# The dilated mixer worked through by head pairs, with its attention two rounds behind its projections

## The reference, cut to what matters

```python
proj = (h @ w_in).reshape(B, S, 3, 3, 16, 64)           # 3 groups; q, k, v; 16 heads of 64
for gi, (window, dilation) in enumerate(((128, 1), (512, 4), (2048, 16))):
    q = rms_norm(proj[:, :, gi, 0], g_q[gi]); k = rms_norm(proj[:, :, gi, 1], g_k[gi])
    v = proj[:, :, gi, 2]
    o, lse = dilated_group(q, k, v, pos, rel_bias[:, gi*16:gi*16+16], window, dilation)
# the three groups are merged by a softmax over their lse: one softmax over all their keys
o = einsum('gbsh,gbshd->bshd', softmax(stack(lses)), stack(outs))
x = x + gate1 * (o.reshape(B, S, 1024) @ w_o)
```

## Time and profile before

| | us |
|---|---|
| median of 3 runs | 2176.52 |
| lowest, highest | 2175.99, 2177.66 |
| the profiled execution, its own time | 2172.89 |
| its span, first to last instruction | 2170.0 |
| busy: PE, PE weight loads, DVE, ACT | 2015.7, 1865.3, 1442.6, 1103.1 |

### The profile page before, as it was taken

One profiled execution on the slowest core, in us unless ns is written; L12 is line 12 of the kernel. 1 busy time (PEld: TensorE's weight loads), 2 busy tenths in 40 slices (PEclk: granted clock), 3 DMA queues, 4 the chain that ended last, 5 costly groups with the idle time before them and its releaser, 6 DMA issues.

```text
span 2170.0 us, 34519 instructions
## 1 busy us (share of the span) xinstructions
PE 2015.7 (93%) x14140; PEld 1865.3 (86%) x14140; DVE 1442.6 (66%) x2525; ACT 1103.1 (51%) x1815; POOL 324.3 (15%) x339
## 2 busy tenths in 40 slices
PE   2758999889999998999889998999999999999998
PEld 1747999889998888999778898999999998888886
DVE  6696785656656655754764545899998775555554
ACT  3544553325655234543555444446777774444444
POOL 3020000000000000000000000004885980000000
PEclk7879999889999789999999999999999999999999
DMA  7534587525545103665432434454444445555553
GB/s 268 190 120 162 196 269 258 193 78 192 195 168 194 35 20 111 203 192 185 176 130 102 146 128 146 174 184 167 154 149 159 144 138 181 186 186 191 186 187 124
DMA packets 97086, 356.22 MB, mean 164 GB/s; under 512 B 10705, under 2 KB 10833, under 8 KB 96545
## 3 DMA queue, kind: packets, MB, share of 16 engines
q1 hardware_dynamic: 83824, 305.04, 40.9%
q0 software_dynamic: 12672, 48.08, 6.9%
q10 hardware_dynamic: 432, 0.90, 0.1%
HBM read 352.93 MB, written 1.05 MB: 163 GB/s over the span
## 4 chain that ended last, share of the span: by engine, by line
PE 83%; DVE 11%; ACT 4%; DMA 1%; issue 1%; SPq 0%; DVEq 0%; POOL 0%; ACTq 0%
PE psum L460 23%; PE psum L461 22%; PE psum L462 22%; PE psum L453 14%; DVE wl L1548 2%; PE psum L467 1%; DVE araw L1531 1%; ACT work L1028 1%; DMA first<-in_ada_w 1%; DVE work L1528 1%; ACT sqh L1028 1%; ACT wh L1040 0%; DVE first L1531 0%; DVE st L1538 0%; DMA araw<-in_ada_w 0%
## 5 line engine op out<-in xcount | busy, mean ns | idle before, releaser
L1548 DVE TENSOR_TENSOR wl<-raw,wh 128x1024 fp32r<-128x1024 f32 (+1 forms) x564 | 688.1, 1226 | 429.9 <-ACT wh L1040 429.3
L1040 ACT ACTIVATE wh<-raw 128x1024 fp32r<-128x1024 f32 (+1 forms) x564 | 592.9, 1053 | 437.0 <-PE psum L462 421.0
L460 PE MATMUL psum<-peer_hh,wh 128*128 128x256 f32 x1152 | 331.0, 287 | 4.2 <-DVE peer_hl L1520 4.0
L461 PE MATMUL psum<-peer_hl,wh 128*128 128x256 f32 x1152 | 326.1, 283 | 0.0
L462 PE MATMUL psum<-peer_hh,wl 128*128 128x256 f32 x1152 | 326.0, 283 | 0.0
L460 PEld LDWEIGHTS psum<-peer_hh,wh 128*128 128x128 f32 x1152 | 219.3, 190 | 5.4 <-issue 4.4
L462 PEld LDWEIGHTS psum<-peer_hh,wl 128*128 128x128 f32 x1152 | 217.2, 189 | 0.0
L461 PEld LDWEIGHTS psum<-peer_hl,wh 128*128 128x128 f32 x1152 | 217.2, 189 | 0.0
L460 PE MATMUL psum<-wh,csh 128*128 128x512 f32 x512 | 202.9, 396 | 0.0
L462 PE MATMUL psum<-wh,csl 128*128 128x512 f32 x512 | 202.7, 396 | 0.0
L461 PE MATMUL psum<-wl,csh 128*128 128x512 f32 x512 | 202.7, 396 | 0.0
(11 more groups left out here) (423 smaller groups left out, 4747.2 us busy)
## 6 DMA issues: line engine op xcount, KB each, us to landing
raw<-in_mlp_w SPq DMA_DIRECT2D x128, 512.0 KB, 4.2
raw<-in_eu SPq DMA_DIRECT2D x128, 512.0 KB, 3.2
raw<-in_ev SPq DMA_DIRECT2D x128, 512.0 KB, 3.2
araw<-in_ada_w POOLq DMA_DIRECT2D x80, 512.0 KB, 4.1
raw<-in_dil_qk SPq DMA_DIRECT2D x48, 512.0 KB, 4.1
raw<-in_dil_v SPq DMA_DIRECT2D x24, 512.0 KB, 4.4
first<-in_ada_w SPq DMA_DIRECT2D x8, 1024.0 KB, 18.1
raw<-in_w_in SPq DMA_DIRECT2D x16, 512.0 KB, 3.3
```

The source lines that it names most:

```text
L460: e.matmul(o, l[0], r[0], start=start, stop=False, skip_group_check=loose)
L461: e.matmul(o, l[0], r[1], start=False, stop=False, skip_group_check=loose)
L1040: e.activation(b.wh[v % NSPLIT][:, 0:cols], b.raw[v % NRAW][:, 0:cols], ACT.Copy).then_inc(S.hi, 1)
L1548: e.tensor_tensor(b.wl[v % NSPLIT][:, 0:cols], b.raw[v % NRAW][:, 0:cols], b.wh[v % NSPLIT][:, 0:cols].bitcast(F32), ALU.subtract).then_in ...
```

## The change

Work is ordered by the eight pairs of heads instead of by groups, by one list (`DIL_ORDER`) that PE, ACT and DVE all follow.
- First come 18 of the 24 value units, with both `bias(0)` and `bias(1)` beside them; `B` holds both query tiles. The other 6 value units come after the last q and k.
- Round c (0 to 7) has the six q and k units of pair c. In rounds 2 to 7 the four attention steps of pair c-2 stand behind its first two units, two behind each. The norm of pair c-1's heads is finished in round c: the three roots are taken in one go, and each of the three q/k banks is scaled by two instructions of 256 columns instead of one of 512.
- Round 8 has the 6 late value units and the norm of pair 7. Then come steps 24 to 34, with units of `dil_w_o` between them. Such a unit now takes the rows of `w_o` that belong to one pair, and adds to all eight output blocks, which keep four PSUM banks; the residual and the squares for the next norm come after the last unit.
- In a step, ACT copies the transposed probabilities first (one buffer, where there were three) and exponentiates second; PE takes `s3` ahead of `s2`.
- The mask is fetched whole by one transfer; ticks have places of their own in the list (31 of them).

```diff
 
 
+def dil_order():
+
+
+    values = [("dil_v", 8 * g + x, x // 2) for g in range(3) for x in range(8)]
+    out = []
+    for i, e in enumerate([e for e in values if e[2] < 3]):
+        out.append(e)
+        if i % 4 == 3:
+            out.append(("tick", 0, 0))
+    out.append(("biased", 0, 0))
+    late = [e for e in values if e[2] == 3]
+
+    def beside(c, z):
+
+        if z % 2 == 0:
+            s, g = (c, z // 2 - 1) if z else (c - 1, 2)
+            if 0 <= s < 8:
+                out.append(("sum", s, g))
+        s, g = {3: (c, 0), 5: (c, 1), 0: (c - 1, 2)}.get(z, (-1, 0))
+        if c and z == 3:
+            out.append(("root", c - 1, 0))
+        if c and z in (3, 4):
+            out.append(("root square", c - 1, z - 3))
+        if c and z == 4:
+            out.append(("root square", c - 1, 2))
+        if 0 <= s < 8:
+            out.append(("mean", s, g))
+        if z % 2 and c < 8:
+            out.append(("square", c, z // 2))
+        if z in (0, 2, 3):
+            out.append(("tick", c, z))
+        if c and z in (3, 4):
+            out.append(("scale", c - 1, z - 3))
+        if c and z == 4:
+            out.append(("scale", c - 1, 2))
+        for u in {0: (4 * c - 8, 4 * c - 7), 1: (4 * c - 6, 4 * c - 5)}.get(z, ()):
+            if 0 <= u < 24:
+                out.append(("step", u, 0))
+
+    for c in range(8):
+        for z in range(6):
+            out.append(("dil_qk", 8 * z + c, z))
+            beside(c, z)
+    for z in range(6):
+        out.append(late[z])
+        beside(8, z)
+    out += [("step", 24, 0), ("step", 25, 0)]
+    tail = [(26,), (27,), (28, 29), (30, 31), (32, 33), (34,), (), ()]
+    for i, steps in enumerate(tail):
+        out += [("step", u, 0) for u in steps] + [("dil_w_o", i, 0)]
+    return out
+
+
+DIL_ORDER = dil_order()
 PLAN = []
...
+    m.qk = sb("qk", 2 * 6 * 256, where=s).rearrange("p (b z t) -> p b z t", b=2, z=6)
+    with ExitStack() as values:
+        m.vtf = sb("vt", 8 * 768, where=values)
+        m.vt = m.vtf.rearrange("p (c g t n) -> p c g t n", c=8, g=3, t=2)
+    m.o = sb("dil_o", 8 * 768, F32R, s).rearrange("p (c x t) -> p c x t", c=8, x=3)
+    m.B = sb("B", 2 * 16 * 512, where=s).rearrange("p (t h n) -> p t h n", t=2, h=16)
+    m.work = sb("work", 2048, where=s)
+    with ExitStack() as early:
+        m.step = sb("step", 1024, F32R, early).rearrange("p (g q) -> p g q", g=8)
+        m.ot = sb("ot", 768, where=early)
+        m.maskc = sb("maskc", 1024, where=early)
+        m.tabs = pair("tabs", 192, early)
+        m.pF = sb("pF", 320, where=early)
+    m.hms = sb("head_means", 4 * 512, where=s).rearrange("p (g n) -> p g n", g=4)
+    m.hrs = sb("head_roots", 3 * 512, where=s).rearrange("p (g n) -> p g n", g=3)
+    sq = [sb("head_squares", 512, where=s) for _ in range(3)]
+    m.hsq, m.hrq = [sq[0], sq[2], sq[2]], [sq[1], sq[0], sq[1]]
...
+            if u % 4 == 0:
+                take("do", c)
+            ps = b.psum[:, at["bank", "do", c], :]
...
+            if u % 4 == 3:
+                give("do", c, sem=S.dve, key=("dil", "out", c))
+
+        def step(i):
             if i < 32:
                 s1(i)
+            if 0 <= i - 3 < 32:
+                s3(i - 3)
             if 0 <= i - 2 < 32:
                 s2(i - 2)
-            if 0 <= i - 3 < 32:
-                s3(i - 3)
-        residual("dil_o", "dil_w_o", m.hh, lambda k: (S.dve, ("dil", "out", 3)), m.work)
+
+        def rows(i):
+            if i == 0:
+                for c2 in range(4):
+                    take("dil_o", c2)
+            j = weights("dil_w_o", i)
+            for c in range(8):
+                o = b.psum[:, at["bank", "dil_o", c // 2], (c % 2) * 256:(c % 2) * 256 + 256]
+                w, x = wsp(j, c * 128, 128), m.o[:, i]
+                first, last = i == 0 and c % 2 == 0, i == 7 and c % 2 == 1
+                mm(o, w[0], x[:, 0, :], first, False, loose=True)
+                mm(o, w[0], x[:, 1, :], False, False, loose=True)
+                if c == 7:
+                    e.matmul(o, w[1], x[:, 0, :], start=False, stop=last, skip_group_check=True).then_inc(S.unit, 1)
+                else:
+                    mm(o, w[1], x[:, 0, :], False, last, loose=True,
+                       mark=("dil_o", "done", c // 2) if last else None)
+
...
+        for c2 in range(4):
+            give("dil_o", c2, sem=S.dve, key=("dil_o", "out", c2))
+            square_sums("dil_o", c2, m.work)
...
+        def step(i):
+            if 0 <= i - 2 < 32:
+                if i >= 3:
+                    ac.wait_ge(S.pe, at["dil", "pv", i - 3])
+                ac.wait_ge(S.pe, at["dil", "turned", i - 2])
+                act(wk[3], bank("dt", i - 2), ACT.Copy, mark=("dil", "probT", i - 2))
             if i < 32:
...
+            if 0 <= i - 3 and (i - 3) % 4 == 3:
+                c = (i - 3) // 4
+                ac.wait_ge(S.pe, at["dil", "pv", i - 3])
+                act(m.o[:, c, 0, :], bank("do", c)[:, 0:256], ACT.Copy, mark=("dil", "o hi", c))
+
...
+            elif kind == "square":
+                ac.wait_ge(S.unit, u + 1)
+                if z == 0 and i >= 2:
+                    ac.wait_ge(S.dve, at["dqk", "out", i - 2, 1])
+                if z == 1 and i >= 1:
+                    ac.wait_ge(S.pe, at["headsum", i - 1, 2])
+                if z == 2:
+                    ac.wait_ge(S.pe, at["headsum", i, 1])
+                act(m.hsq[z], bank("dqk", i, z), ACT.Square, mark=("head square", i, z))
+            elif kind == "mean":
+                past = 3 * i + z - 4
+                if past >= 0:
+                    ac.wait_ge(S.dve, at["dqk", "out", past // 3, past % 3])
+                ac.wait_ge(S.pe, at["headsum", i, z])
+                act(m.hms[:, (past + 4) % 4, :], bank("headsum", i, z), ACT.Identity, scale=1.0 / 64, bias=eps,
+                    mark=("headsum", "ms", i, z))
+            elif kind == "root":
+                ac.wait_ge(S.act, n[0])
+                if i:
+                    ac.wait_ge(S.dve, at["dqk", "out", i - 1, 2])
+                for g in range(3):
+                    act(m.hrs[:, g, :], m.hms[:, (3 * i + g) % 4, :], ACT.Abs_reciprocal_sqrt, mark=("root", i, g))
+            elif kind == "root square":
+                ac.wait_ge(S.act, at["root", i, z])
+                if z == 0 and i:
+                    ac.wait_ge(S.dve, at["dqk", "out", i - 1, 2])
+                if z == 1 and i < 7:
+                    ac.wait_ge(S.pe, at["headsum", i + 1, 0])
+                if z == 2:
+                    ac.wait_ge(S.dve, at["dqk", "out", i, 0])
+                act(m.hrq[z], m.hrs[:, z, :], ACT.Square, mark=("head rs0", i, z))
...
+        for c2 in range(4):
+            square("dil_o", c2, m.work, ("dil_o", "out", c2))
...
+        side = chain(bias(0), bias(1))
+
+        def head_norm(c, g):
+            sq, ms, y = m.hrq[g], m.hms[:, (3 * c + g) % 4, :], m.hrs[:, g, :]
+            ve.wait_ge(S.act, at["head rs0", c, g])
+            stt(sq, ms, -0.5, sq, ALU.mult, ALU.mult)
+            own()
+            stt(sq, sq, 1.5, y, ALU.add, ALU.mult)
+            own()
+            if c >= 2:
+                ve.wait_ge(S.pe, at["dil", "scores", 4 * (c - 2) + 3])
+            ps = bank("dqk", c, g)
+            for x, gain in enumerate(("dil_g_q", "dil_g_k")):
+                z = slice(256 * x, 256 * x + 256)
+                stt(m.qk[:, c % 2, 2 * g + x, :], ps[:, z], vc(b, gain, g), sq[:, z], ALU.mult, ALU.mult,
+                    mark=("dqk", "out", c, g))
...
+        for c in range(8):
+            if c < 6:
+                ve.wait_ge(S.pe, at["dil_o", "done", c // 2])
+            else:
+                ve.wait_ge(S.unit, u + 1)
+            xs = b.xT[:, c * 256:c * 256 + 256]
+            stt(xs, bank("dil_o", c // 2)[:, (c % 2) * 256:(c % 2) * 256 + 256], b.mod[:, 64 + c:65 + c], xs, ALU.mult,
+                ALU.add, mark=("dil_o", "out", c // 2))
...
+        e.dma_start(m.maskc, d["mask"]).then_inc(S.mask, 16)
+        tick(sum(kind == "tick" for kind, i, z in DIL_ORDER))
+        mod_until(80)
```

More of the change, by code:

```diff
@@ L2 @@
 from contextlib import ExitStack
+from itertools import chain
 import numpy as np
@@ L209, in plan @@
     add("mlp_w2", 32)
-    for g in range(3):
-        add("dil_qk", 16, first=16 * g)
-        add("dil_v", 8, first=8 * g)
-    add("dil_w_o", 8)
+    for kind, i, j in DIL_ORDER:
+        if kind in ("dil_v", "dil_qk", "dil_w_o"):
+            add(kind, 1, first=i)
     add("mlp_w1", 32, first=32)
@@ L760, in dilated @@
         phase("dil")
-        side = bias(0)
-        rings = [0, 3]
-        wait_n = []
-        def head_sums(zi, c2):
-            ps = take("headsum", zi, c2)
-            w = rings[(4 * zi + c2) % 2]
-            pe.wait_ge(S.act, at["head square", zi, c2])
-            mm(ps, blk, m.work[:, w * 512:w * 512 + 512], True, True, mark=("headsum", zi, c2))
-            give("headsum", zi, c2, sem=S.act, key=("headsum", "ms", zi, c2))
```

(48 more changed lines are left out.)

237 lines of the change are left out of this document (69 added, 168 removed).

## The result

The changed kernel takes 2137.84 us (median of 4 runs, 2137.69 to 2142.64) against 2176.26 (4 runs, 2172.28 to 2177.66) for the kernel before on the same chip: ratio 0.9832, 95% interval 0.9813 to 0.9851. The profiled executions differ by less: 2172.89 and 2137.76, which is 35.1 us. The other 3.3 come from the kernel before, whose profiled execution was a quick one.

What follows compares the result with a forecast made beforehand. It took TensorE to bound attention and projections alike, leaving only low clock and waits to gain; the terms summed to -25.2 us, so 2176.5 - 25.2 = 2151.3 us, range 2140 to 2172.

Steps and rivals of the forecast that it cites:

- clock: Whole stage: loss from TensorE running at the low clock falls from 37.6 to 11.4 us, -26.2 us.
- waits: Whole stage: TensorE's waits for other engines fall from 15.8 to 12.6 us, -3.2 us.
- changes of kind: Attention steps set between units at 19 places: each switch of TensorE work costs 0.08 us, +3.0 us.
- squares: End of stage: squares of three of four column pairs no longer lie between the units on TensorE, -2.0 us.
- end of stage: After the last matmul: residual additions, squares and a bare table load delay the last sums, +3.7 us.
- start: Start of the stage: the first unit needs only half of the normalised input, -0.5 us.
- 1 us a round: Rounds 2 to 7: TensorE waits from the strict order of hand-overs, 6 us in all, bounds 0 and 3 a round.
- Clock as beside the first bias: Rival: in the values the clock falls as often as beside bias(0), 24 us lost for 8: 2167; chance 0.15.
- Rounds bound by hand-overs: Rival: ScalarE and VectorE hand-overs add 3 us a round, and as much in late values: 2165; chance 0.11.
- Slower: Rival: low clock through most of the values, 75 of 94 us of work at half clock: 2218; chance 0.10.
- milder case: Same rival as "Slower", with half of the values' work at the low clock: 2190; no chance of its own.
- Does nothing: Rival: overlapping attention and projections gives nothing, clock and hand-overs take back the 25 us: 2176; chance 0.06.

Runs made afterwards that it cites:

- repeat: The changed kernel profiled and timed once more with no edit: 2139.32 us, ratio 0.9842, stage 402.6 us.
- bunched kernel: The changed kernel with a round's four attention steps behind one unit instead of two and two behind two units: 2144.5 us, ratio 0.9857.
- table kernels: The changed kernel with Identity in place of the exponential in the dilated mixer's steps, so no table loads in the rounds: 2135.2 us, ratio 0.9808.
- `bias(1)` alone: The changed kernel with bias(1) worked off alone behind the 18 value units, bias(0) still beside them: 2154.65 us, ratio 0.9896.
- one place was right here and two were not: Changed kernel, pause filled, unit between bias(1)'s last gathers, table early, pair 7 scaled earlier in round 8: one place 2126.74 us, two places 2132.77 us.

## Why the prediction was wrong

The sign and the mechanism held, and the size did not. By the terms of the sum, with both profiles of the changed kernel (stage -33.1 and -37.8 us):

| term | forecast | first profile | repeat |
|---|---|---|---|
| clock | -26.2 | -22.3 | -27.4 |
| waits | -3.2 | -11.4 | -12.1 |
| changes of kind | +3.0 | 0 | 0 |
| squares | -2.0 | -2.0 | -2.0 |
| end of stage | +3.7 | +3.4 | +3.4 |
| start | -0.5 | -0.1 | 0 |
| sum | -25.2 | -32.4 | -38.1 |

*Clock* (time at half / 2, from 75.1 us to 30.6 and 20.4). Right in kind: values at full clock in 0.8 and more of their length, `bias(1)` no longer low, which is 13.7 us when undone by itself. "One fall after the first pause and one or two in the eight own steps" is what the first profile has, 8.5 us for 8 in the values. What the forecast did not have is the fall in round 8, 3.4 us, which stands behind the step-25 wait: a wait was priced at its own length, without the fall that follows it.

*Waits*, the step that failed. The forecast has 12.6 us left, of which 4.4 (3.7 in the repeat) exist. 6 us of it were "1 us a round", and there is nothing: the strict order was followed with every engine's work at its highest, 25 us of VectorE and 23 of ScalarE a round, where rounds 3 to 7 have 22.1 and 20.7 (on VectorE 11 rows of the condition's product in five rounds, not 15), and with the roots, scalings, split and tick all ahead of the first step's bias. "The probabilities that TensorE wants are ready within 0.1 us" was 2.0 us in the step read above. The bunched kernel shows that, once the pipeline is full, even four steps in a row make no wait. The length of a round was right, 30.6 for 31, but all of it is TensorE's work. Round 8 cost 3.0 for 4.6, at the place foreseen; the tail 0.75 for 1.4; the values 0.7 for 0.6.

*Changes of kind*. TensorE's busy time in the stage, with the time lost to the clock taken off, is 418.5 - 37.6 = 380.9 us before and 396.2 - 15.3 = 380.9 after. The squares are in both. So 38 changes cost nothing in sum. The rounds show why it is not 0.08 us each: four steps cost 30.63 - 19.74 = 10.89 us beside units, for 4 x 2.68 = 10.72 alone, so a round loses 0.17 us and not the 0.32 of four changes. The timeline above shows where it comes back: the four transposes hold TensorE for 0.58 us ahead of scores (592.02 to 592.60) and 0.41 ahead of a unit (594.69 to 595.10). With the old order in a step, which doesn't end on them, a round is another 0.17 us longer. The sum of 0 needs the 1.0 us that six rounds lose to be saved elsewhere in the stage; where was not measured.

*End, squares, start*. +3.4 for +3.7, with the table load bare between the squares as foreseen (816.25), worth 1.3 us by experiment. The half input at the start gave nothing: TensorE's 4.1 us wait ahead of the stage is the same before and after.

*From the stage to the time*. 7.9 of the 13.5 us between 2151.3 and 2137.8 are the terms above, 2.0 outside the stage, and 3.5 the offset of median and profiled execution, which was 3.6 us before and 0.1 after. I had carried the 3.6 over as if it belonged to the kernel. Waits, kinds and this offset all erred to the same side, and the range's low end, 11 us below the forecast, did not hold them together.

*The rivals*. "Clock as beside the first bias" (24 us lost) did not come: 8.5 and 3.4 in the values. "Rounds bound by hand-overs" is ruled out for rounds 3 to 7 by the bunched and the table kernels. "Slower" did not come; the units brought the clock back each time, and without them (`bias(1)` alone) 37.5 us stay low. (By its own terms the rival's milder case, half of the work low, was 2151.3 + 37.5 - 8 = 2181, not 2190.) "Does nothing" failed for the reason given in the forecast: overlap of two TensorE-bound parts gives nothing by itself, but it takes away the bare stretches. On the tables, the Trainium skill ("ScalarE: Activation LUTs", "Rules for kernel authors") wants one set done before a switch. The 14 loads are there, 18.0 us in all at 1283 ns, and the kernel without them has rounds of the same length, 30.63 us. By the page, as the forecast estimates from it, up to 17 us were at stake; the trace does not agree for this order, since ScalarE has 9.9 us of slack a round.

## What to carry to other kernels

When two parts are bound by the same engine, laying them beside each other gains by what stood bare in either: here narrow matmuls alone (at half clock) and the end of a chain of vector work. Price each wait of TensorE with the fall of the clock that may follow (3.4 us for each fall of 6.8 here), and a wait of under 1 us ahead of narrow matmuls is worth filling. Take the wait you forecast in a steady loop from the busy sums (22.1 and 20.7 of 30.6 us leave room), and keep the median apart from the profiled execution; and when a task is moved ahead on a full engine, look at what it is moved past, since one place was right here and two were not.

## What the runs showed that was not expected

- The same program had stages of 407.3 and 402.6 us in two profiles, because 1.3 us more at the low clock at its start hid a pause of 0.67 us, whose falls had cost 5.1 us.
- Falls come behind pauses of 0.67 us (at 425.5, fall at 428) and 3.0 us (765, fall at 766), and amid narrow matmuls that run from 511.4 to 519.9 without a pause or a unit (517). With four attention steps in a row one fall came as a wait of 1.6 us in the first bunch ended (568), and none in the later ones, which have no wait. Not every wait has a fall: the 0.75 us in the tail (799) and the 1.07 us ahead of the sums (814) had none behind them.
- A table load is 1.28 us and the next ACTIVATE starts 0.02 us behind it (816.25 + 1.28 = 817.53; 817.55), so it has no drain there that the profile shows.
